# A last FFN step in two passes, and mixer bodies in five groups with whole units

## What is computed

```python
def half_step_ffn(x, g_pre, g_post, w_gu, w_down):
    h = rms_norm(x, g_pre)
    gate, up = jnp.split(h @ w_gu, 2, axis=-1)
    y = (jax.nn.silu(gate) * up) @ w_down
    return x + 0.5 * rms_norm(y, g_post)
...
    xp = half_step_ffn(xp, ffn1_pre_g[l], ffn1_post_g[l], ffn1_w_gu[l], ffn1_w_down[l])
    q, k, v, hq, hk, logf, hv, hg = mixer_inputs(rms_norm(xp, mix_pre_g[l]) @ w_in[l], pos_p, lb_all[l])
    att, nk, nv = swa_prompt(q, k, v, attn_sinks[l])
    ho, S_p = hgrn2_prompt(hq, hk, logf, hv)
    xp = xp + rms_norm(mixer_output(att, ho, hg, hgrn_out_g[l], w_out[l]), mix_post_g[l])
    xp = half_step_ffn(xp, ffn2_pre_g[l], ffn2_post_g[l], ffn2_w_gu[l], ffn2_w_down[l])
```

## Time and profile before

| | us |
|---|---|
| three timed runs | 2111.83, 2115.23, 2116.56 |
| median | 2115.23 |
| the profiled execution | 2110.59 |
| its span, first to last instruction | 2108.8 |
| TensorE busy in it | 2046.0 (97%) |
| VectorE busy | 1097.2 (52%) |
| ScalarE busy | 581.0 (28%) |
| GpSimd busy | 69.4 (3%) |

### The profile page before, as it was taken

The page is one execution under the profiler, slowest core; times in us unless marked ns, Lnnn a source line. Parts: engine busy times, 40 slices in busy tenths (PEclk is TensorE's granted clock), DMA queues, the critical chain, the costliest instruction groups (busy, mean ns, idle before and its releaser), DMA issues.

```text
span 2108.8 us, 33511 instructions
## 1 busy us (share of the span) xinstructions
PE 2046.0 (97%) x13575; PEld 1979.0 (94%) x13575; DVE 1097.2 (52%) x1927; ACT 581.0 (28%) x952; POOL 69.4 (3%) x34
## 2 busy tenths in 40 slices
PE   5999999999999998999999999999999999999996
PEld 5999999999999987998888899999999999999995
DVE  4543444444444467566666668644434444444446
ACT  5211111211111134145555655411111112111112
POOL 3000000000000003000000110100000000000000
PEclk9999999999999999999999999999999999999998
DMA  3211111111111113110010154111111111111111
GB/s 123 61 51 50 39 41 50 50 40 50 50 50 50 34 31 147 40 33 31 21 31 21 63 198 160 54 51 51 50 50 40 40 50 50 40 50 50 50 31 80
DMA packets 30127, 118.53 MB, mean 56 GB/s; under 512 B 3552, under 2 KB 4456, under 8 KB 28136
## 3 DMA queue, kind: packets, MB, share of 16 engines
q1 hardware_dynamic: 30056, 117.52, 17.2%
HBM read 106.67 MB, written 10.83 MB: 56 GB/s over the span
## 4 chain that ended last, share of the span: by engine, by line
PE 92%; DVE 4%; ACT 2%; issue 1%; DMA 0%; SPq 0%; DVEq 0%; ACTq 0%
PE PS L375 25%; PE PS L376 25%; PE PS L377 25%; PE PS L506 2%; PE PS L507 2%; PE PS L508 2%; PE PS L552 2%; PE PS L698 1%; DVE resid L1355 1%; PE PS L413 1%; PE PS L700 1%; PE PS L699 1%; DVE y L1350 1%; DVE x_lo L1363 1%; ACT sm L1119 1%
## 5 line engine op out<-in xcount | busy, mean ns | idle before, releaser
L375 PE MATMUL PS<-x_hi,w_hi 128*128 128x344 f32 x2280 | 733.0, 321 | 32.3 <-DVE w_lo L1337 22.0
L376 PE MATMUL PS<-x_lo,w_hi 128*128 128x344 f32 x2280 | 728.8, 320 | 0.0
L377 PE MATMUL PS<-x_hi,w_lo 128*128 128x344 f32 x2280 | 727.7, 319 | 0.0
L375 PEld LDWEIGHTS PS<-x_hi,w_hi 128*128 128x128 f32 x2280 | 429.5, 188 | 34.7 <-issue 21.9
L376 PEld LDWEIGHTS PS<-x_lo,w_hi 128*128 128x128 f32 x2280 | 429.6, 188 | 1.0
L377 PEld LDWEIGHTS PS<-x_hi,w_lo 128*128 128x128 f32 x2280 | 429.7, 188 | 0.0
L1454 DVE TENSOR_TENSOR y<-y,PS 128x344 f32<-128x344 f32 x528 | 264.4, 511 | 182.2 <-PE PS L377 182.2
L375 PE MATMUL PS<-h,w_hi 128*128 128x344 f32 x1056 | 339.7, 322 | 0.0
L376 PE MATMUL PS<-h,w_hi 128*128 128x344 f32 x1056 | 337.6, 320 | 0.0
L377 PE MATMUL PS<-h,w_lo 128*128 128x344 f32 x1056 | 336.7, 319 | 0.0
L895 ACT ACTIVATE w_hi<-raw 128x1024 fp32r<-128x1024 f32 x156 | 161.4, 1049 | 468.3 <-PE PS L377 464.2
(11 more groups left out here) (217 smaller groups left out, 1852.6 us busy)
## 6 DMA issues: line engine op xcount, KB each, us to landing
raw<-in_w_gu SPq DMA_DIRECT2D x88, 512.0 KB, 3.6
raw<-in_w_down SPq DMA_DIRECT2D x44, 512.0 KB, 3.6
raw<-in_w_in SPq DMA_DIRECT2D x22, 512.0 KB, 3.6
raw<-in_w_out SPq DMA_DIRECT2D x19, 512.0 KB, 3.7
resid<-in_x SPq DMA_DIRECT2D x3, 1376.0 KB, 9.3
stream_x<-resid SPq DMA_DIRECT2D x3, 1376.0 KB, 5.3
resid<-stream_x SPq DMA_DIRECT2D x3, 1376.0 KB, 7.8
out_y<-resid SPq DMA_DIRECT2D x3, 1376.0 KB, 4.7
```

Source lines behind the costliest of these rows:

```text
L375: nc.tensor.matmul(PS[:, bank, :GW], wh, vh, start=(k == 0), stop=False)
L376: nc.tensor.matmul(PS[:, bank, :GW], wh, vl, start=False, stop=False)
L377: mm = nc.tensor.matmul(PS[:, bank, :GW], wl, vh, start=False, stop=(k == last))
```

## The change

It touches four places.

**The input.** `vecs` is loaded first, then the first weight tile, then group 0 of x in two halves; the identity and `head_ones` come after the rest of x. ScalarE loads its table at once and splits the first weight before x. TensorE starts on feature tile k of x as soon as `x0_low` shows its low part. The folds of the squares go from GpSimd to VectorE, and the first FFN step copies to y instead of adding to zeros, so that the memsets of y are gone.

**The last step of both FFNs.** It is two passes over its six weight tiles, which are loaded and split twice (`again`). Pass one takes group 0 alone: four gate and up units, then its eight down units (three of them in two halves of three matmuls). Pass two takes groups 1 and 2. Group 0 of y is squared, summed, scaled, added and (after FFN 1) split for the next projection during pass two; in FFN 1 its square of x is summed before the down units of group 2, and the sum of group 1 of y stands within those. Group 2 of y is squared and summed in two parts (`half_sum`).

**The rest of the border.** y is scaled and added by halves of four feature tiles (`scaled_half`, `added_half`), x is split by halves, and the store of y at the end of the kernel goes by halves too. The squares of group 1 of x aren't folded any more (`S`, 1, 1).

**The bodies.** Dense units are whole, at five places. TensorE's body is: outputs and second attention of the body before, level 0, first masks and scores, level 1, dense; level 2, second masks and scores, level 3, dense; level 4, keys, dense; states, first transposed probabilities, dense; first attention, second transposed probabilities, dense. ScalarE and VectorE are reordered to it. The scan of body 0, its differences and first decayed products are made with tiles 7 and 8.

```diff
-G_IN = FFN_STEPS * FFN_GRANULES
+G_IN = (FFN_STEPS + 1) * FFN_GRANULES
...
-            sp.dma_start(resid[:, 0], ins["x"][0]).then_inc(resid_full[0], 16)
-            sp.dma_start(vecs[:], ins["vecs"]).then_inc(S["consts_in"], 16)
...
+            sp.dma_start(vecs[:], ins["vecs"]).then_inc(S["vecs_in"], 16)
...
             load(0, 0, ins["w_gu1"][0])
+            sp.dma_start(resid[:, 0, 0:KT // 2], ins["x"][0][:, 0:KT // 2]).then_inc(S["x0_in"], 16)
+            sp.dma_start(resid[:, 0, KT // 2:], ins["x"][0][:, KT // 2:]).then_inc(resid_full[0], 16)
             load(1, 1, ins["w_gu1"][1])
...
+            def again(n0, w_gu, w_down):
+
+                for o in range(4):
+                    load(n0 + 6 * FFN_STEPS + o, o % 3, w_gu[4 * (FFN_STEPS - 1) + o])
+                for o in range(2):
+                    load(n0 + 6 * FFN_STEPS + 4 + o, 1 + o, w_down[2 * (FFN_STEPS - 1) + o])
...
+                for o in range(4):
+                    gate_up(0, o, 0, o)
+                pe.wait_ge(S["w_ready"], READY_CREDIT + n + 6)
+                pe.wait_ge(S["h_lo_done"], step_h + 1)
+                for m in range(3):
+                    down_half(0, m, 4 + m, 0)
+                pe.wait_ge(S["h_lo_done"], step_h + 2)
+                for m in range(3):
+                    down_half(0, m, 4 + m, 1)
+                for m in range(3, KT):
+                    down_tile(0, m, 4 + m)
+                for o in range(4):
+                    for g in range(1, NG):
+                        gate_up(1, o, g, 12 + 2 * o + g - 1)
+                        if (o, g) == (1, 1):
+                            norm_sum(("F", b, 0))
+                pe.wait_ge(S["w_ready"], READY_CREDIT + n + 12)
+                pe.wait_ge(S["h_lo_done"], step_h + 5)
+                for m in range(KT):
+                    down_tile(1, m, 20 + m)
+                if b == 0:
+                    norm_sum(("S", 1, 0))
+                pe.wait_ge(S["h_lo_done"], step_h + 6)
+                for m in range(KT):
+                    down_tile(2, m, 28 + m)
+                    if m == 5:
+                        norm_sum(("F", b, 1))
...
+            half_sum(0, 0)
+            pe.wait_ge(S["x_split_lo"], NG + 1)
+            pair_unit(G_IN, U_IN, 0, 0)
+            half_sum(0, 1)
+            pair_unit(G_IN, U_IN, 0, 1)
+            pe.wait_ge(S["x_split_lo"], NG + 2)
+            pair_unit(G_IN, U_IN, 1, 0)
+            pair_unit(G_IN, U_IN, 1, 1)
+            norm_sum(("S", 1, 1))
+            pair_unit(G_IN, U_IN, 2, 0, x1_ready)
+            norm_sum(("S", 1, 2))
+            pair_unit(G_IN, U_IN, 2, 1)
...
-                dense(0)
+                ahead()
                 level(0)
-                dense(1)
+                masks(0)
+                scores(0)
+                level(1)
                 if b == 0:
                     values()
...
+                dense(0)
                 level(2)
-                dense(3)
+                masks(1)
+                scores(1)
+                level(3)
...
+                dense(1)
+                level(4)
+                keys_by_token()
+                dense(2)
+                states()
+                probs_by_key(0)
+                dense(3)
+                attend(0)
+                probs_by_key(1)
                 dense(4)
...
-            border_pool(-1)
-            nc.gpsimd.memset(y[:], 0.0).then_inc(S["y_zero"], 1)
-            border_pool(0)
...
+                gate(1, 16)
+                added_half(b, 0, 1)
+                gate(2, 17)
+                split_lo(n + 11, 2)
+                if b == 0:
+                    low_half(b, 0, 0, None)
+                up(1, 18, 5)
+                h_low(1, 1, 5)
+                if b == 0:
+                    low_half(b, 0, 1, S["x_split_lo"])
+                up(2, 19, 6)
+                h_low(2, 1, 6)
...
                 if i:
                     unit_end(4, i - 1)
+                decayed(i, 2)
+                if i:
                     weights_low(4, i - 1)
-                else:
+                weights(0)
+                sub_max(0)
+                weights(1)
```

More of the change, by code:

```diff
@@ L434, in ffn, with step @@
             def ffn(n0, u0, f, b):
-                def step(i, first, last):
+                def step(i, first):
                     u, step_h = u0 + 36 * i, 6 * FFN_STEPS * f + 6 * i
@@ L517, in head_sums, with body @@
                 mm.then_inc(S["css_done"], 1)
[L519 removed]
+            def body(i, ahead):
                 t, b, c = i // 2, i % 2, i
@@ new lines, in low_half @@
+            def low_half(b, g, a, done):
+                for m in range(KT // 2 * a, KT // 2 * (a + 1)):
+                    dve.wait_ge(S["x_split_hi"], KT * (NG * (b + 1) + g) + m + 1)
+                    low = nc.vector.scalar_tensor_tensor(x_lo[:, g, m], resid[:, g, m], vecs[:, PRE[b] + m:PRE[b] + m + 1],
+                                                         x_hi[:, g, m].bitcast(F32), ALU.mult, ALU.subtract)
+                if done is not None:
+                    low.then_inc(done, 1)
@@ new lines, in ffn @@
+                for m in range(KT):
+                    down(2, m, 28 + m)
+                    if m == 4:
+                        fold(("F", b, 1))
+            split_lo(0, 0)
+            for m in range(KT):
+                dve.wait_ge(S["x_split_hi"], m + 1)
+                nc.vector.scalar_tensor_tensor(x_lo[:, 0, m], resid[:, 0, m], vecs[:, PRE[-1] + m:PRE[-1] + m + 1],
+                                               x_hi[:, 0, m].bitcast(F32), ALU.mult, ALU.subtract)\
+                    .then_inc(S["x0_low" if m < KT - 1 else "x_split_lo"], 1)
```

670 lines of the change are left out of this document (400 added, 270 removed).

## The result

The changed kernel takes 2076.12 us (median of four runs, 2075.86 to 2076.69); the kernel before, run beside it, 2113.53 (2110.64 to 2116.56). The ratio is 0.982, with a 95% interval of 0.981 to 0.984. The forecast was 2075, in a range of 2062 to 2090. The profiled execution of the changed kernel has a span of 2074.9 us, so 33.9 us less than that of before; the sum of the prediction was 38.8.

A forecast was written before the change was run, and what follows sets the result against it. The prediction took TensorE, busy for 2046.0 of 2108.8 us, as the bound. Its terms, 13.9 + 7.0 + 15.1 + 2.8 = 38.8 us, gave 2071.8 from the profiled execution or 2076.4 from the median; it forecast 2075, range 2062 to 2090.

The forecast's parts named there:

- all four parts gain: Main case: start, last step and border, bodies and tail each save time, 38.8 us together; chance 0.79.
- The start: Start of the kernel: TensorE's first product at 7.5 to 8 us, not 22.0; gain 13.9 us, bounds 12 and 15.5.
- Last step and border: First FFN's end to the input projection: 15.4 us of waits and clock falls removed, 8.4 added; net gain 7.0 us.
- Bodies: Eight mixer bodies: 9.5 us of waits removed, 7.6 saved on entries, 2.0 of new waits; net gain 15.1 us.
- Merged entries: Mixer bodies: whole dense units save 39 entries at some 0.2 us each, 7.6 us in all.
- four places are the whole sum: Whole kernel: only start, first FFN border, bodies and tail change; FFN loops between stay as they are; 38.8 us.
- Tail: End of the kernel: two groups left in halves and a smaller store save 7.9 us, 5.1 added; net gain 2.8.
- A: Rival, bodies: they keep as much waiting as they lose, at new places; 7.5 us less gain, 2083; chance 0.12.
- B: Rival, pass one: it starves on weights, 12.8 us a layer in place of 1.4; 2098; chance 0.03.
- C: Rival, bodies: VectorE falls one group behind, 51 us of waits in place of 2; 2124, slower; chance 0.03.
- E: Rival, front of the kernel: first data land no earlier and the rest cancels; within 0.2%; chance 0.01.
- D: Rival, bodies: the clock falls in each body, 1.7 us a fall, 13.6 in all; 2089; chance 0.02.

The follow-up runs named there:

- warm_start: Changed kernel with 14 small products of ones by ones in front of TensorE's first unit, while it waits for the first data; 2075.54 us against 2076.1.
- border_order: Changed kernel with three places of the new last step and border put in another order, nothing added or removed; 2070.37 us against 2076.1.
- cut_units: Changed kernel with each of the bodies' 39 dense units cut in two halves again, a small element between the halves; 2082.98 us against 2076.1.
- states_beside: Changed kernel with further reorderings (2064.22 us), altered by moving the states' products one group later in every body, ahead of the attention's first products; 2061.66 us.
- window_late: Changed kernel with the load of the samples' value window issued behind that of the third out-projection weight, not in front; 2073.92 us against 2076.1.
- old_bodies: Changed kernel with the early tiles and bodies of the kernel before put back, all else staying changed; 2088.63 us against 2076.1.

## Why the prediction was right, and where it was off

**The whole.** 2075 forecast, 2076.1 measured, and its case (all four parts gain) is the one that came. The nearness is partly luck. The sum was 38.8, and the gain is 37.4 by the medians of the runs beside each other, 33.9 between the two profiled executions. The profile of before was 4.6 us under the median that the forecast started from, that of the changed kernel is the longest of its four runs, 0.6 above their median. What came less what was forecast, by stage in the table's order: -0.9, -0.2, +1.4, -3.2, -2.3, +0.3, together -4.9. (One bound of the prediction doesn't come out of its own terms: two parts at their low end, with 4 + 7.1 us less, give 2086 to 2088, not 2090.)

**The start.** First product at 8.13, forecast 7.5 to 8.1: the walk held. From there to the end of the stretch the changed kernel took 27.85 us and the kernel before 26.99, so the term was 0.9 too large: the low clock lasted 5.1 us in that execution, where it was 3.2 in before's, and at 0.47 us for each us more that is the 0.9. The sum had counted the earlier first product alone and took what follows it for unchanged. That taking it away altogether gains little is what warm_start showed; then the walk's margins on VectorE (x_lo, w_lo, folds) are the bound.

**Last step and border.** Forecast waits 1.4 in pass one; measured 0.23 + 0.37. Pass two 1.35 + 2.1; measured 1.29 + 0.27 + 0.84. Fold of F1 1.35; 1.17. x_lo of group 1 0.75; 0.50. Fold of S(1,2) 1.4; 1.43. Each wait came, with its releaser, 6.1 us in place of 8.35, and border_order took them away by the orders that the prediction had blamed. Two terms were mis-sized: pass one (1.4, measured 0.6) and the two short waits of pass two (2.1, measured 1.1). Both falls of the clock went with the long waits.

**Bodies.** The waits went from 9.55 to 1.25 (forecast 2.0, of which 0.6 + 0.4 in body 0; measured 0.81 + 0.44, and none later, where I had allowed 1 us more). Merged entries: 7.6 forecast, 6.7 by cut_units. The mean was nearly right, but the prediction had read 0.2 at entries from and to levels and put it on all 39; a cut by a transpose costs 0.08. What failed is that no price stood in the sum for the elements that got new neighbours: that inside a group "only masks (0.53) and scores (1.02)" stand between two levels was read for time, not for what follows what. A change of the array's shape costs 0.07 to 0.15 us (cut_units, states_beside), the new order has five more in a body, and it is 0.37 us a body dearer than the old at equal cuts, 3.0 us. 8.3 + 6.7 - 3.0 = 12.0, and 11.9 was measured.

**Out-projection.** The prediction's "four places are the whole sum" failed here by 2.3 us in the first profiled execution and by 0.7 in the second. Moving outputs() and attend(1) behind the last unit moved the moment at which SyncE may load the samples' data closer to that of the next weight, and of a step that is moved every load that hangs on its neighbours should have been followed. It was 1.0 of wait (window_late), which both have, and in the first 1.7 of clock, less some tenths; what brings that fall on in one execution and not in the other stays open.

**Tail.** 2.8 forecast, 3.1 measured. The halves took 14.4 us on VectorE, the store 3.0 instead of 3.8.

**Rivals.** A (bodies keep as much waiting) fell: none in seven bodies. B (pass one starves): 0.6 us of waits in place of 12.8. C (VectorE a group behind) fell with A. E fell with the first product. D, the clock in the bodies, didn't come true in the changed kernel, but the sentence that argued against it, that the clock falls to 0.50 "only after waits of over 4 us", was wrong: old_bodies shows a fall right behind 1.83 us, and the out-projection one 20 us behind the last wait. The rule of the Trainium skill that was weighed there, that short idles between groups can be enough, has one case on its side, the fall in old_bodies; the same wait in the kernel before had none behind it, and no run tells whether the wait was the cause.

## What to carry to other kernels

When small products are reordered between large ones, price each border by its kind: an entry into the large unit cost 0.08 us here where the array kept its shape, and each change of shape 0.07 to 0.15 us more (0.17 for a mean entry, which holds both). Count the changes of shape in the new order, and keep kinds of one shape side by side. When a stage's last steps are moved, list the loads that wait for each of them: here two moments came 1.2 us closer, a weight took 1.0 us longer to land, and TensorE waited 1.0 us in a stage that nobody had touched. And a wait that a walk along an in-order queue predicts can often be taken away by one exchange in that queue; three such exchanges were worth as much as half of the bodies' rebuilding.

## What the runs showed of the hardware

- A change of the tile shape between neighbouring products costs TensorE time: 0.15 us between 128\*64 and 128\*128 (states_beside), 0.07 as a mean of all kinds of change (cut_units against the kernel before). At every change, those with 64\*128 and 64\*64 too, the weight load starts with its product, not ahead of it. A small run of the same shape as the large products costs only 0.08 us when it parts them.
- The clock can fall to 0.50 behind a wait of 1.83 us (old_bodies, 6.8 us at 0.50, 3.2 lost), and the same wait in the kernel before left it at 1.00. It can fall behind 2 us of tiny products without a wait right in front (3.4 us at 0.50, 1.7 lost; a wait of 1.0 to 1.5 us stood 17 us ahead of the products each time), in one execution of a program and not in another.
- Starts of the same instructions showed 3.6 to 6.2 us at the low clock, and each us beyond the first 3.6 cost 0.47 us; 5.5 us of small products ahead of them removed it, with a gain too small to tell, since the other engines were the bound then.
- 512 KB landed 7.1 us after issue behind 2.5 MB of loads issued in the 4.1 us before (the samples' 2 MB and one weight), 5.8 behind 2 MB; the usual 512 KB load landed after 3.6.
